# Gate of the first layer summed in one bank, and x1 turned over a diagonal, in a two-layer fp32 diffusion trunk

## The chip, the cores and the metric

The kernel runs on one core of one Trainium2 chip. The metric is the device time of one execution in microseconds, as a median of several runs. A profiled execution gives the trace; its times count from the start of its span.

## What is computed

Two layers work on 512 tokens of 1024 features in fp32. The first mixes tokens by averaging windows of 2, 4, 8 and 16 tokens, the second by a short gated convolution; after each comes a squared-ReLU MLP. Each sub-layer has an RMS norm before and after it, a shift and scale, and a gate; the six vectors of a layer are SiLU(c) times a 1024 x 6144 matrix, plus a bias.

```python
for i in range(DEPTH):                      # DEPTH = 2
    sh_m, sc_m, gt_m, sh_f, sc_f, gt_f = split(silu(c) @ ada_w[i] + ada_b[i], 6)
    h = rms_norm(x, norm_g[i, 0]) * (1 + sc_m) + sh_m
    y = pool_mixer(h) if i == 0 else short_conv_mixer(h)
    x = x + gt_m * rms_norm(y, norm_g[i, 1])          # "x1" in layer 0
    hf = rms_norm(x, norm_g[i, 2]) * (1 + sc_f) + sh_f
    x = x + gt_f * rms_norm(square(relu(hf @ ffn_w1[i])) @ ffn_w2[i], norm_g[i, 3])
```

## The kernel before

The engines' programs are written out by hand, each in one block; semaphores order them, and each engine runs its block strictly in the order written. So the order of calls in the code is the order on the engine.

Large products are made in three TensorE matmuls (`three`, lines 674 to 676): each fp32 operand is split into a high part, which ScalarE writes by a copy that rounds (`split_hi`, `first_hi`), and a low part, which VectorE makes by a subtraction (`split_lo`, `first_lo`). Weights come as units of 1 MB through two raw slots, by DMAs of the SP queue.

The change lies in the first 90 us or so, in which layer 0's mixer, its gate and the MLP's first inputs are made:

- **The modulation vectors.** `PRE` lists 20 loads of 1 MB of `ada_w[0]`, in order: eight for scale and shift of the mixer, four for the gate (numbers 8 to 11), eight for scale and shift of the MLP (12 to 19). Each load takes a quarter (256 columns) of one vector's 1024, for all 1024 input rows. A partition holds eight input rows, so its rows in memory are 1 KB. `PRE_SLOTS` says where in SBUF each load goes. `add_up(i)` multiplies load i by SiLU(c) on TensorE: eight matmuls, each with 32 output rows, four side by side. `SUMS` says which loads are summed into one PSUM bank; two banks (`sums_bank`) alternate.
- **The gate.** `gate_copy(part)` on VectorE adds bias and weight (`g_row`, which GpSimd prepares with a multiplication) to one quarter's sum; `turn_up(4 + part)` on TensorE spreads it over the partitions with the table `picks`; `group_gate(g)` on VectorE multiplies the quarter g of the mixer's output, for all tokens, by it.
- **The mixer.** `pool_group(g)` on TensorE makes the output of one group of 256 features, `group_out(g)` on VectorE copies it from PSUM to `y_tok`, `group_squares(g)` on ScalarE sums its squares. `split_lo(1)` on VectorE, the low part of the first MLP unit, stands between them.
- **x1 and its norm.** `first_x(t)` on VectorE makes x1 of tile t (128 tokens), `first_root(t)` on ScalarE its root mean square, `first_norm(t)` on VectorE multiplies all 1024 columns by the reciprocal and writes them to `y_tok`. `turn_first(side, pair)` on TensorE transposes four blocks of 128 x 128 of it (`nc.tensor.transpose`, line 955). It is called eight times, between `add_up`, `turn_up` and `part` in `start_pairs`.
- **The first inputs.** `first_input`, `first_hi` and `first_lo` scale, shift and split what was turned; `part(side, pair)` and `second_unit`, `third_unit` are the MLP's first products. `columns(n)` puts a quarter of scale and shift in place.
- **x stored.** `save_x(0)` on the SP queue writes x1 to memory before the load of unit 4; `load_x_parts`, which loads weights over `xs`, waits for it.
- `stay_busy` is six matmuls of a 128 x 128 identity that nobody reads.

Of the kernel before, what the change touches and what calls it, by code (L numbers as in the profile page):

```python
# [10 lines left out]
P = 128  # L11
# [77 lines left out]
PRE = ([(s, c) for c in range(4) for s in (SCALE_M, SHIFT_M)] + [(GATE_M, c) for c in range(4)]  # L89
# [3 lines left out]
SUMS = [(2 * c, 2 * c + 1) for c in range(4)] + [(PRE_GATE + c,) for c in range(4)] + [(PRE_F + 2 * c, PRE_F + 2 * c + 1) for c in range(4)]  # L93
# [42 lines left out]
def trunk(nc, x, c, ada_w, ada_b, norm_g, ffn_w1, ffn_w2, pool_w, pool_scale, conv_in_w, conv_w, conv_out_w, out):  # L136
    with ExitStack() as ctx:  # L137
# [60 lines left out]
        picks = sb("picks", [P, P])  # L198
# [37 lines left out]
        gate_bias = sem("gate_bias")  # L236
# [12 lines left out]
        x1_new, x1_sq, x1_rms, x1_rcp, x1_norm = sem("x1_new"), sem("x1_sq"), sem("x1_rms"), sem("x1_rcp"), sem("x1_norm")  # L249
# [33 lines left out]
        def pre_slot(i):  # L283
# [4 lines left out]
            return slot.rearrange("p (k n) -> p k n", k=NC)  # L288
# [234 lines left out]
        def _(sp):  # L523
# [15 lines left out]
            def load_pre(i):  # L539
# [10 lines left out]
                sp.dma_start(pre_slot(i), ada_rows(0)[:, :, seg * D + part * Q:seg * D + (part + 1) * Q]).then_inc(pre_in[PRE_SLOTS[i]], 16)  # L550
# [121 lines left out]
        def _(pe):  # L672
# [192 lines left out]
            def add_up(i):  # L865
# [20 lines left out]
            def turn_up(n):  # L886
                row = ada_rows_sb[:, n % 2, 0:Q]
                if is_gate(n):
                    part = n - 4
                    pe.wait_ge(gate_sums, part + 1)  # L890
                    if part >= 2:
                        pe.wait_ge(y0_gated, part - 1)
                    mm = nc.tensor.matmul(ps[:, 6 + part % 2, 0:Q], picks[:, :], row, start=True, stop=True)
                else:
                    pe.wait_ge(ada_row, cols_value(n))
                    for e in range(2):
                        mm = nc.tensor.matmul(ps[:, sums_bank(n), Q + 2 * e:Q + 2 * e + 2], row[:, e * P:(e + 1) * P], pick_two[:, :], start=True, stop=True)
# [44 lines left out]
            def turn_first(side, pair):  # L942
                pe.wait_ge(x1_norm, 2 * side + 2)
                pe.wait_ge(y0_gated, GROUPS)
# [8 lines left out]
                for n in range(2):  # L953
                    for t in range(2):
                        tr = nc.tensor.transpose(o[:, n, toks(t)], y_tok[:, 2 * side + t, (2 * pair + n) * P:(2 * pair + n + 1) * P], ident[:, :])
                tr.then_inc(x1_turned, 1)

            def start_pairs():
# [35 lines left out]
                turn_up(9)  # L994
                turn_first(1, 2)
                turn_up(10)
# [10 lines left out]
                turn_up(11)  # L1007
# [55 lines left out]
            turn_up(4)  # L1063
            pool_group(3)
            turn_up(5)
            add_up(10)
            add_up(11)
            turn_up(6)
            turn_up(7)
# [3 lines left out]
            turn_up(8)  # L1073
# [23 lines left out]
        def _(act):  # L1097
# [274 lines left out]
            copy_sums(11)  # L1372
# [46 lines left out]
        def _(dve):  # L1419
# [302 lines left out]
            dve.wait_ge(picks_step, 3)  # L1722
# [413 lines left out]
```

## Time and profile before

| | us |
|---|---|
| median of 3 runs | 938.18 (937.9 to 939.74) |
| the profiled execution | 937.01 |
| its span | 935.1 |
| TensorE busy in the span | 914.9 (98%) |
| VectorE busy | 649.3 (69%) |
| ScalarE busy | 431.1 (46%) |
| GpSimd busy | 53.2 (6%) |

The span is the time from the first to the last recorded instruction; 1.9 us of the profiled execution lie around it. The busy share of TensorE says little by itself, since the ends of matmuls are modelled: whether TensorE is the limit of a stretch is read from the starts of its matmuls and from what it waited for. DMA moves 170.86 MB in all, 41.88 MB of them in the first 140 us.

### The profile page before, as it was taken

The page shows a single profiled execution, that of the slowest core. Times are in us where ns is not written, and L with a number is a line of the kernel's source. Part 1 is how long each engine was busy: PE and PEld are TensorE (multiplying, and loading weights), DVE is VectorE, ACT ScalarE, POOL GpSimd, SP SyncE. Part 2 cuts the span into 40 slices and gives each one's busy share as a digit, 9 for nine tenths or more (in the row PEclk, how much of TensorE's full clock was granted, in tenths as well). Part 3 has the DMA queues.
Part 4 walks back from the last instruction along what each step waited for, and adds up shares of the span by engine and source line. Part 5 has one row for each costly group of instructions (what it writes and reads, how often), then busy time and mean ns, then how long its engine had stood idle before and what let it go on. Part 6 is the DMA issues. An engine that isn't in the chain of part 4 may idle for free.

```text
span 935.1 us, 11415 instructions
## 1 busy us (share of the span) xinstructions
PE 914.9 (98%) x4623; PEld 753.6 (81%) x4623; DVE 649.3 (69%) x622; ACT 431.1 (46%) x523; POOL 53.2 (6%) x83
## 2 busy tenths in 40 slices
PE   8889999999999999999999999999999999999996
PEld 6658888888888888889888888898888888888885
DVE  6786397589678866696766545757857864783688
ACT  6654484454346333354222224555634624543463
POOL 3002110010001001000101000000000000000001
PEclk9999999999999999999999999999999999999999
DMA  9999889527735576324656531273871661275124
GB/s 306 349 350 359 210 220 327 183 74 215 256 114 139 187 288 226 112 90 158 209 179 217 194 113 46 84 276 123 238 270 34 169 214 57 72 204 174 45 46 179
DMA packets 91403, 170.86 MB, mean 183 GB/s; under 512 B 4270, under 2 KB 34066, under 8 KB 91352
## 3 DMA queue, kind: packets, MB, share of 16 engines
q1 hardware_dynamic: 83912, 155.25, 48.5%
q0 software_dynamic: 7440, 14.89, 8.1%
q8 instruction: 36, 0.59, 0.3%
q14 instruction: 15, 0.12, 0.0%
HBM read 163.81 MB, written 6.32 MB: 182 GB/s over the span
## 4 chain that ended last, share of the span: by engine, by line
PE 52%; DVE 1%; issue 1%; ACT 0%; DVEq 0%
PE ps L674 17%; PE ps L676 17%; PE ps L675 17%; PE ps L768 1%; DVE y L1580 0%; DVE in_lo L1591 0%; PE ps L703 0%; DVE y L1945 0%; DVE xs L1956 0%; ACT in_hi L1209 0%; DVE y L1586 0%; DVE y L1474 0%; DVEq L137 0%; DVE y L1543 0%; DVE st L1949 0%
## 5 line engine op out<-in xcount | busy, mean ns | idle before, releaser
L674 PE MATMUL ps<-in_hi,w_parts 128*128 128x512 f32 (+1 forms) x784 | 290.1, 370 | 0.9 <-DVE in_lo L1591 0.5
L675 PE MATMUL ps<-in_lo,w_parts 128*128 128x512 f32 (+1 forms) x784 | 288.1, 367 | 0.0
L676 PE MATMUL ps<-in_hi,w_parts 128*128 128x512 f32 (+1 forms) x784 | 288.1, 367 | 0.0
L1422 DVE TENSOR_TENSOR w_parts<-raw,w_parts 128x2048 fp32r<-128x2048 f32 x81 | 185.5, 2290 | 125.5 <-ACT w_parts L1102 125.4
L1102 ACT ACTIVATE w_parts<-raw 128x2048 fp32r<-128x2048 f32 x81 | 154.8, 1911 | 214.4 <-PE ps L676 194.4
L674 PEld LDWEIGHTS ps<-in_hi,w_parts 128*128 128x128 f32 x784 | 147.8, 188 | 29.4 <-issue 3.3
L676 PEld LDWEIGHTS ps<-in_hi,w_parts 128*128 128x128 f32 x784 | 147.8, 188 | 24.5
L675 PEld LDWEIGHTS ps<-in_lo,w_parts 128*128 128x128 f32 x784 | 147.8, 189 | 24.1
L674 PE MATMUL ps<-w_parts,ops_hi 128*128 128x512 f32 x280 | 109.1, 389 | 0.2 <-DVE y L1474 0.2
L675 PE MATMUL ps<-w_parts,ops_hi 128*128 128x512 f32 x280 | 109.0, 389 | 0.0
L676 PE MATMUL ps<-w_parts,ops_lo 128*128 128x512 f32 x224 | 87.2, 389 | 0.0
L1432 DVE SCALAR_TENSOR_TENSOR ada_sum<-ada_raw,silu_t,ada_sum 128x1024 f32<-128x1024 f32 x56 | 71.7, 1281 | 4.7 <-DMA ada_raw<-in_ada_w_dram 2.2
L1112 ACT ACTIVATE work<-ps 128x512 f32<-128x512 f32 x56 | 33.3, 595 | 70.9 <-PE ps L676 70.9
L674 PEld LDWEIGHTS ps<-w_parts,ops_hi 128*128 128x128 f32 x280 | 52.6, 188 | 11.5 <-DVE y L1474 0.7
L675 PEld LDWEIGHTS ps<-w_parts,ops_hi 128*128 128x128 f32 x280 | 52.6, 188 | 10.9
L1474 DVE TENSOR_TENSOR y<-y,ps 128x512 f32<-128x512 f32 x82 | 52.9, 680 | 8.3 <-PE ps L676 8.3
L1422 DVE TENSOR_TENSOR w_parts<-xs,w_parts 128x2048 fp32r<-128x2048 f32 x21 | 48.0, 2285 | 3.3 <-ACT w_parts L1102 3.1
L1102 ACT ACTIVATE w_parts<-xs 128x2048 fp32r<-128x2048 f32 x21 | 40.3, 1919 | 21.6 <-PE ps L676 19.2
L674 PE MATMUL ps<-w_parts,mid_hi 128*128 128x512 f32 x128 | 50.1, 392 | 0.0
L676 PE MATMUL ps<-w_parts,mid_lo 128*128 128x512 f32 x128 | 49.8, 389 | 0.0
L675 PE MATMUL ps<-w_parts,mid_hi 128*128 128x512 f32 x128 | 49.8, 389 | 0.0
L676 PEld LDWEIGHTS ps<-w_parts,ops_lo 128*128 128x128 f32 x224 | 42.0, 188 | 8.7
(203 smaller groups left out, 1040.2 us busy)
## 6 DMA issues: line engine op xcount, KB each, us to landing
raw<-in_ffn_w_dram SPq DMA_DIRECT2D x57, 1024.0 KB, 5.5
ada_raw<-in_ada_w_dram SPq DMA_DIRECT2D x56, 512.0 KB, 6.2
xs<-in_ffn_w_dram SPq DMA_DIRECT2D x14, 1024.0 KB, 5.4
xs<-in_ffn_w_dram POOLq DMA_DIRECT2D x10, 1024.0 KB, 8.7
raw<-in_conv_in_w_dram SPq DMA_DIRECT2D x16, 512.0 KB, 5.3
raw<-in_ada_w_dram SPq DMA_DIRECT2D x4, 1024.0 KB, 11.1
ada_sum<-in_ada_w_dram SPq DMA_DIRECT2D x4, 1024.0 KB, 12.2
win<-in_ada_w_dram SPq DMA_DIRECT2D x4, 1024.0 KB, 11.9
```

What stands on the lines that cost most here:

```text
L674: nc.tensor.matmul(o, hi, b_hi, start=start, stop=False, skip_group_check=on)
L675: nc.tensor.matmul(o, hi, b_lo, start=False, stop=False, skip_group_check=on)
L676: return nc.tensor.matmul(o, lo, b_hi, start=False, stop=stop, skip_group_check=on)
L768: tr = nc.tensor.transpose(ps[:, at + n // 4, (n % 4) * P:(n % 4 + 1) * P], y_tok[:, t, n * P:(n + 1) * P], ident[:, :])
L1102: nc.scalar.activation(w_hi[:, u % W_SLOTS, :], raw_of(u), ACT.Copy).then_inc(w_hi_ready, 1)
L1112: nc.scalar.activation(work[:, n % 2, :], bank(p, m), ACT.Relu).then_inc(relu_done, 1)
L1422: nc.vector.tensor_tensor(w_lo[:, u % W_SLOTS, :], raw_of(u), w_hi[:, u % W_SLOTS, :].bitcast(F32), ALU.subtract).then_inc(w_lo_ready, 1)
L1432: nc.vector.scalar_tensor_tensor(out=ada_sum[:, s % 2, :], in0=ada_raw[:, i % ADA_SLOTS, :], scalar=silu_t[:, 3, k:k + 1], in1=ada_sum[:, ...
L1474: nc.vector.tensor_tensor(to, to, src, ALU.add if sign > 0 else ALU.subtract).then_inc(y_sum, 1)
```

## The change

Five things are changed.

1. The gate's four loads now take 256 of the 1024 input rows each, for all 1024 columns: `(GATE_M, kk)` is the pair of input rows `2*kk, 2*kk+1` of each partition, in rows of 4 KB. All four are summed in one bank, quarter j of the columns in the output rows from 32 j on. Four small matmuls add the bias to the sum at its start.
2. One VectorE operation (`weigh_gate`) multiplies the sum by the weight, after the fourth load; `spread_gate` on TensorE (four fp32 matmuls of 128 x 256) spreads it over banks 6 and 7; `token_gate(t)` on VectorE multiplies a tile of 128 tokens by it, over all 1024 columns. `gate_copy`, four of the `turn_up`, `group_gate`, `picks` and GpSimd's multiplication go.
3. `first_norm` becomes `first_diag`: the identity (128 columns) times the reciprocal. `turn_first` is now a matmul with a block of x1 as the stationary and this diagonal as the moving operand, so that it turns and scales in one.
4. On VectorE `first_x(3)` stands ahead of the first `columns` and `first_input`; on ScalarE `first_root(3)` ahead of `first_hi(0)`. `first_diag(2)` and `first_diag(3)` stand around `first_lo(0)`.
5. `save_x(0)` comes after the load of unit 4 and waits for all eight `turn_first`, which now read x1.

```diff
-PRE = (... + [(GATE_M, c) for c in range(4)] ...
+PRE = (... + [(GATE_M, kk) for kk in range(4)] ...
-SUMS = [...] + [(PRE_GATE + c,) for c in range(4)] + [...]
+SUMS = [...] + [tuple(range(PRE_GATE, PRE_F))] + [...]
...
+                if seg == GATE_M:
+                    sp.dma_start(pre_slot(i), ada_rows(0)[:, 2 * part:2 * part + 2, seg * D:(seg + 1) * D]).then_inc(pre_in[PRE_SLOTS[i]], 16)
...
+                if n == GATE_SUM:
+                    if first:
+                        pe.wait_ge(gate_row_in, 16)
+                        for j in range(4):
+                            nc.tensor.matmul(ps[32 * j:32 * (j + 1), sums_bank(n), 0:Q], ones[0:1, 0:32], gate_row[0:1, quarter(j)], start=True, stop=False)
+                    for k in range(2):
+                        for j in range(4):
+                            mm = nc.tensor.matmul(ps[32 * j:32 * (j + 1), sums_bank(n), 0:Q], silu_wide[:, 1, 2 * PRE[i][1] + k, :], pre_slot(i)[:, k, quarter(j)],
+                                                  start=False, stop=last and k == 1)
...
+            def spread_gate():
+                pe.wait_ge(gate_sums, 1)
+                pe.wait_ge(pool_diff, BAND_CHUNK + 2)
+                for j in range(4):
+                    mm = nc.tensor.matmul(ps[:, 6 + j // 2, (j % 2) * Q:(j % 2 + 1) * Q], ident[:, 32 * j:32 * j + 1].to_broadcast([P, P]), g_row[:, 0:Q], start=True, stop=True)
...
             def turn_first(side, pair):
-                pe.wait_ge(x1_norm, 2 * side + 2)
-                pe.wait_ge(y0_gated, GROUPS)
+                pe.wait_ge(x1_diag, 2 * side + 2)
+                pe.wait_ge(y0_gated, NT)
...
-                        tr = nc.tensor.transpose(o[:, n, toks(t)], y_tok[:, 2 * side + t, (2 * pair + n) * P:(2 * pair + n + 1) * P], ident[:, :])
+                        tr = nc.tensor.matmul(o[:, n, toks(t)], xs[:, 2 * side + t, (2 * pair + n) * P:(2 * pair + n + 1) * P], y_tok[:, 2 * side + t, 0:P], start=True, stop=True)
...
-            def gate_copy(part):
-                n = 4 + part
...
-                nc.vector.scalar_tensor_tensor(out=ada_rows_sb[:, n % 2, 0:Q], in0=ps[:, sums_bank(n), 0:Q], scalar=ident[:, 0:1],
-                                               in1=g_row[:, quarter(part)], op0=ALU.add, op1=ALU.mult).then_inc(gate_sums, 1)
+            def weigh_gate():
+                dve.wait_ge(ada_done, PRE_F)
+                dve.wait_ge(gate_g_in, 16 * 4)
+                nc.vector.tensor_tensor(g_row[:, 0:Q], ps[:, sums_bank(GATE_SUM), 0:Q], g_row[:, 0:Q], ALU.mult).then_inc(gate_sums, 1)
...
-            def group_gate(g):
...
+            def token_gate(t):
+                dve.wait_ge(ada_turned, GATE_SUM + 1)
+                dve.wait_ge(y0_sq, NT * (GROUPS - 1) + t + 1)
+                yt = y_tok[:, t, :].rearrange("p (a n) -> p a n", a=2)
+                nc.vector.tensor_tensor(yt, yt, ps[:, 6:8, :], ALU.mult).then_inc(y0_gated, 1)
...
-                nc.vector.tensor_scalar(y_tok[:, t, :], xs[:, t, :], st0[:, 7, t:t + 1], None, ALU.mult).then_inc(x1_norm, 1)
+                nc.vector.tensor_scalar(y_tok[:, t, 0:P], ident[:, :], st0[:, 7, t:t + 1], None, ALU.mult).then_inc(x1_diag, 1)
```

On TensorE, from the second half of the gate's sums to the wait for the first turn, the program before has (`L877` is `add_up`, `L893` and `L897` are `turn_up`, `L884` is `stay_busy`, `cu` holds SiLU(c) and the copied sums):

```order
L893 MATMUL ps<-cu,picks 128x256 [waits gate_sums]
L877 MATMUL ps<-mod_rows,cu 32x256 [waits gate_sums,pre_in3]
L877 MATMUL ps<-mod_rows,cu 32x256 x7
L877 MATMUL ps<-raw,cu 32x256 [waits gate_sums,pre_in6]
L877 MATMUL ps<-raw,cu 32x256 x7
L893 MATMUL ps<-cu,picks 128x256 [waits y0_gated,gate_sums] x2
L877 MATMUL ps<-win,cu 32x256 [waits gate_sums,pre_in7]
L877 MATMUL ps<-win,cu 32x256 x7
L877 MATMUL ps<-win,cu 32x256 [waits pre_in8]
L877 MATMUL ps<-win,cu 32x256 x7
L884 MATMUL ps<-ident,ones 128x128 x6
L897 MATMUL ps<-pick_two,cu 128x2 [waits ada_row]
```

The changed program has there, in the same place (`L883` is `add_up` of the gate, `L910` `spread_gate`):

```order
L883 MATMUL ps<-mod_rows,cu 32x256 [waits pre_in3]
L883 MATMUL ps<-mod_rows,cu 32x256 x7
L883 MATMUL ps<-raw,cu 32x256 [waits pre_in6]
L883 MATMUL ps<-raw,cu 32x256 x7
L910 MATMUL ps<-ada_raw,ident 128x256 [waits pool_diff,gate_sums]
L910 MATMUL ps<-ada_raw,ident 128x256 x3
L889 MATMUL ps<-win,cu 32x256 [waits cols_read,pre_in7]
L889 MATMUL ps<-win,cu 32x256 x7
L889 MATMUL ps<-win,cu 32x256 [waits pre_in8]
L889 MATMUL ps<-win,cu 32x256 x7
L896 MATMUL ps<-ident,ones 128x128 x6
L902 MATMUL ps<-pick_two,cu 128x2 [waits ada_row]
```

The four spreading matmuls of the gate, which stood apart, are now one group behind the last of its loads.

On VectorE, from the output of the third group to the first x1, the program before has (`L1800` is `group_out`, `L1795` `gate_copy`, `L1808` `group_gate`, `L1422` `split_lo(1)`, `L1813` `first_x`):

```order
L1800 TENSOR_TENSOR y<-ps,pool_row 128x4x256 [waits pool_done]
L1795 SCALAR_TENSOR_TENSOR cu<-ps,ident,ada_raw 128x256 [waits gate_g_in,gate_bias,ada_turned,ada_done]
L1808 TENSOR_TENSOR y<-y,ps 128x4x256 [waits y0_sq,ada_turned]
L1422 TENSOR_TENSOR w_parts<-raw,w_parts 128x2048 [waits w_hi_ready]
L1800 TENSOR_TENSOR y<-ps,pool_row 128x4x256 [waits pool_done]
L1808 TENSOR_TENSOR y<-y,ps 128x4x256 [waits y0_sq,ada_turned]
...
L1808 TENSOR_TENSOR y<-y,ps 128x4x256 [waits y0_sq,ada_turned]
L1883 RECIPROCAL st<-st 128x4 [waits y0_rms]
L1808 TENSOR_TENSOR y<-y,ps 128x4x256 [waits y0_sq,ada_turned]
L1813 SCALAR_TENSOR_TENSOR xs<-y,st,xs 128x1024 [waits y0_gated,y0_rcp] x3
```

The changed program has (`L1804` is `group_out`, `L1800` `weigh_gate`, `L1812` `token_gate`, `L1432` `split_lo(1)`, `L1817` `first_x`, `L1824` `first_diag`):

```order
L1804 TENSOR_TENSOR y<-ps,pool_row 128x4x256 [waits pool_done]
L1432 TENSOR_TENSOR w_parts<-raw,w_parts 128x2048 [waits w_hi_ready]
L1804 TENSOR_TENSOR y<-ps,pool_row 128x4x256 [waits pool_done]
L1800 TENSOR_TENSOR ada_raw<-ps,ada_raw 128x256 [waits gate_g_in,ada_done]
L1812 TENSOR_TENSOR y<-y,ps 128x1024 [waits y0_sq,ada_turned] x2
L1879 TENSOR_TENSOR st_y<-st_y 128x4x2 [waits y0_sq]
L1881 TENSOR_TENSOR st<-st_y 128x4 [waits y0_sum]
L1812 TENSOR_TENSOR y<-y,ps 128x1024 [waits y0_sq,ada_turned] x2
L1885 RECIPROCAL st<-st 128x4 [waits y0_rms]
L1817 SCALAR_TENSOR_TENSOR xs<-y,st,xs 128x1024 [waits y0_gated,y0_rcp] x3
L1822 RECIPROCAL st<-st 128x1 [waits x1_rms]
L1824 TENSOR_SCALAR y<-ident,st 128x128 [waits x1_rcp]
```

Two of the four multiplications by the gate stood before or beside the output of the last group; all four now stand behind it, and behind `weigh_gate`.

## Rows read from the trace of the kernel before

**Rows 1.** The page: busy time by engine.

```profile
PE 914.9 (98%) x4623; PEld 753.6 (81%) x4623; DVE 649.3 (69%) x622; ACT 431.1 (46%) x523; POOL 53.2 (6%) x83
```

**Rows 2.** Waits of PE (TensorE) from 110 to 420 us: total, times, longest.

```profile
PE ps L674 <- DVE y L1474: 0.2, 1, 0.2
```

**Rows 3.** Stretches: length, PE, PEld, DVE, ACT, POOL busy, clock, DMA share, GB/s.

```profile
79.00:90.00 11.00, 11.00 (x79) 9.28 (x78) 6.91 (x12) 3.76 (x4) 4.94 (x8) 1.00 0.96 368
...
40.00:55.00 15.00, 12.92 (x134) 8.89 (x123) 14.26 (x23) 10.29 (x31) 0.00 (x0) 1.00 1.08 350
84.00:86.00 2.00, 2.00 (x12) 1.68 (x10) 0.54 (x1) 1.43 (x3) 1.59 (x3) 1.00 1.01 409
...
6.00:8.00 2.00, 2.00 (x3) 0.76 (x3) 1.86 (x19) 1.96 (x4) 0.32 (x1) 1.00 1.03 416
```

**Rows 4.** Timeline of PE, gate to first turn: start, duration, line, records, [idle before].

```profile
50.41 0.59 PE L893 MATMUL ps<-cu,picks 128*128 128x256 f32 x2
...
52.77 1.07 PE L877 MATMUL ps<-raw,cu 128*32 128x256 f32 x16 [0.78 <-DMA raw<-in_ada_w_dram]
...
59.04 1.07 PE L877 MATMUL ps<-win,cu 128*32 128x256 f32 x16 [1.95 <-DMA win<-in_ada_w_dram]
60.04 1.60 PE L884 MATMUL ps<-ident,ones 128*128 128x128 f32 x12
61.83 0.61 PE L897 MATMUL ps<-pick_two,cu 128*128 128x2 f32 x4 [0.19 <-ACT cu L1273]
62.80 0.66 PE L955 MATMUL ps<-ident,y 128*128 128x128 f32 x4 [0.36 <-DVE y L1820]
```

**Rows 5.** Timeline of DVE (VectorE), same stretch and columns.

```profile
46.10 1.22 DVE L1800 TENSOR_TENSOR y<-ps,pool_row 128x1024 f32<-128x1024 f32 x1
...
51.07 1.22 DVE L1800 TENSOR_TENSOR y<-ps,pool_row 128x1024 f32<-128x1024 f32 x1
52.20 1.21 DVE L1808 TENSOR_TENSOR y<-y,ps 128x1024 f32<-128x1024 f32 x1
...
54.44 0.48 DVE L1795 SCALAR_TENSOR_TENSOR cu<-ps,ident,ada_raw 128x256 f32<-128x256 f32 x1
54.84 1.21 DVE L1808 TENSOR_TENSOR y<-y,ps 128x1024 f32<-128x1024 f32 x1
...
57.35 3.67 DVE L1813 SCALAR_TENSOR_TENSOR xs<-y,st,xs 128x1024 f32<-128x1024 f32 x3
...
61.99 0.75 DVE L1820 TENSOR_SCALAR y<-xs,st 128x1024 f32<-128x1024 f32 x1
```

**Rows 6.** Timeline of ACT (ScalarE): high part of unit 1, root of tile 1.

```profile
46.85 1.90 ACT L1102 ACTIVATE w_parts<-raw 128x2048 fp32r<-128x2048 f32 x1
...
61.21 0.30 ACT L1316 ACTIVATE st<-st,eps 128x1 f32<-128x1 f32 x1
```

**Rows 7.** Timeline of PE, first turns to the first whole unit; columns as in rows 4.

```profile
66.06 0.39 PE L674 MATMUL ps<-in_hi,w_parts 128*128 128x256 f32 x1
...
70.13 1.09 PE L955 MATMUL ps<-ident,y 128*128 128x128 f32 x8
71.16 1.07 PE L877 MATMUL ps<-win,cu 128*32 128x256 f32 x16
...
82.94 0.50 PE L674 MATMUL ps<-in_hi,w_parts 128*128 128x512 f32 x1
```

**Rows 8.** Timeline of PE: one window of the mixer, four plain fp32 matmuls.

```profile
17.72 1.18 PE L927 MATMUL ps<-bands,xn_tok 128*128 128x132 f32 x8
18.83 1.07 PE L877 MATMUL ps<-y,cu 128*32 128x256 f32 x16
```

**Rows 9.** Timeline of PE at the end: its last matmul.

```profile
926.23 0.39 PE L676 MATMUL ps<-w_parts,ops_lo 128*128 128x512 f32 x1
```

**Rows 10.** A stretch behind it, columns as in rows 3.

```profile
931.00:932.00 1.00, 0.00 (x0) 0.00 (x0) 0.96 (x4) 0.00 (x0) 0.00 (x0) 0.68 0.69 258
```

**Rows 11.** Timeline of the SP queue: the loads that wait for the store of x.

```profile
89.33 1.06 SPq L621 DMA_DIRECT2D xs<-in_ffn_w_dram  x2
```

More of the change, by code:

```diff
@@ L887, in turn_up @@
                 row = ada_rows_sb[:, n % 2, 0:Q]
[L888 to L897, printed above, removed]
+                pe.wait_ge(ada_row, cols_value(n))
+                for e in range(2):
+                    mm = nc.tensor.matmul(ps[:, sums_bank(n), Q + 2 * e:Q + 2 * e + 2], row[:, e * P:(e + 1) * P], pick_two[:, :], start=True, stop=True)
+                mm.then_inc(ada_turned, 1)
+            def spread_gate():
+                pe.wait_ge(gate_sums, 1)
+                pe.wait_ge(pool_diff, BAND_CHUNK + 2)
+                for j in range(4):
+                    mm = nc.tensor.matmul(ps[:, 6 + j // 2, (j % 2) * Q:(j % 2 + 1) * Q], ident[:, 32 * j:32 * j + 1].to_broadcast([P, P]), g_row[:, 0:Q], start=True, stop=True)
                 mm.then_inc(ada_turned, 1)
@@ L1006, in start_pairs @@
                 second_unit(2)
-                turn_up(11)
+                turn_up(8)
                 second_unit(3)
@@ L1062, in _ @@
             add_up(9)
-            turn_up(4)
             pool_group(3)
-            turn_up(5)
             add_up(10)
             add_up(11)
-            turn_up(6)
-            turn_up(7)
+            spread_gate()
             add_up(PRE_F)
@@ L1072, in _ @@
             stay_busy(0, 6)
-            turn_up(8)
+            turn_up(5)
             ffn(0)
@@ L1371, in _ @@
             split_hi(3)
-            copy_sums(11)
+            copy_sums(8)
             first_hi(4)
@@ L1750, in columns @@
             def columns(n):
-                part = n % 4
-                late = n >= 8
+                late = n > GATE_SUM
+                part = n - GATE_SUM - 1 if late else n
                 c = slice(2 * part, 2 * part + 2)
@@ L1863, in _ @@
             diff_lo(5)
-            gate_copy(0)
             diff(6)
@@ L1869, in _ @@
             group_out(2)
-            gate_copy(1)
-            group_gate(0)
             split_lo(1)
             group_out(3)
-            group_gate(1)
-            gate_copy(2)
+            weigh_gate()
+            token_gate(0)
+            token_gate(1)
             dve.wait_ge(y0_sq, NT * GROUPS)
@@ L1879, in _ @@
             nc.vector.tensor_tensor(st0[:, 2, :], st_y[:, :, 0], st_y[:, :, 1], ALU.add).then_inc(y0_sum, 1)
-            gate_copy(3)
-            group_gate(2)
+            token_gate(2)
+            token_gate(3)
             dve.wait_ge(y0_rms, 1)
             nc.vector.reciprocal(st0[:, 4, :], st0[:, 3, :]).then_inc(y0_rcp, 1)
-            group_gate(3)
             first_x(0)
@@ L1887, in _ @@
             first_x(2)
-            first_norm(0)
-            first_norm(1)
-            columns(8)
+            first_diag(0)
+            first_diag(1)
+            first_x(3)
+            columns(5)
             first_input(0)
+            first_diag(2)
             first_lo(0)
-            first_x(3)
-            first_norm(2)
-            first_norm(3)
+            first_diag(3)
             first_input(1)
-            columns(9)
+            columns(6)
             first_lo(1)
@@ L1901, in _ @@
             first_lo(2)
-            columns(10)
+            columns(7)
             first_input(3)
@@ L1907, in _ @@
             split_lo(3)
-            columns(11)
+            columns(8)
             first_input(5)
```

68 lines of the change are left out of this document (27 added, 41 removed).

## The prediction

> **What bounds the kernel now.** I read the page first: TensorE is busy 98% of the span [rows 1]. Its waits come next, since busy time alone proves nothing here: from 110 to 420 us it waits 0.2 us in all [rows 2], and from 79 to 90 us it has no idle time [rows 3]. So from the first turn of x1, at 62.80 us [rows 4], TensorE runs without a gap, and two things decide the time: **when that turn starts, and how much TensorE has to do behind it**. Ahead of it two others set the pace. The 16 DMA engines are full, 350 GB/s at a share of 1.08 from 40 to 55 us [rows 3]; TensorE waits 0.78 us for the last load of the gate and 1.95 us for load 13 [rows 4]. And VectorE is busy 14.26 of these 15 us [rows 3]. The chain into the first turn is: add_up of the last gate load at 52.77 [rows 4], its copy at 54.44, the third and fourth multiplication by the gate from 54.84 on, first_x from 57.35 on [rows 5], the root of tile 1 until 61.51 [rows 6], its norm until 62.74 [rows 5], the turn at 62.80 [rows 4].
>
> **The loads.** A load is 1.05 MB. At 350 GB/s it takes 3.00 us. No row shows 4 KB rows alone; the nearest are the stretch with x's own loads, which have rows of 4 KB, at 416 GB/s, and one with weights in rows of 2 KB and the store of x, at 409 [rows 3]. At 409 a load takes 2.56 us, so the fourth gate load lands 4 x 0.44 = 1.8 us sooner, at about 51.0. Bounds: nothing gained (52.7), or 1.9 us at 416. Not all of it can be used. pool_group(3) holds TensorE until 50.4 (the next matmul starts at 50.41 [rows 4]), add_up(10) follows, 1.0 us, so add_up(11) starts at 51.4 instead of 52.77 and is done at 52.45. The bias matmuls, at most 0.5 us by add_up's 16 records in 1.07 [rows 4], stand ahead of pool_group(2) and push it by 0.1. GpSimd's multiplication and `picks` go from work that nobody waits for: nothing.
>
> The Trainium skill (DMA: Bandwidth & Descriptors, "Where 436 GB/s comes from") has it that transfers from HBM are held at about 358 GB/s by the HBM's side, whatever their rows. The trace does not agree: 409 and 416 in two stretches of full DMA [rows 3]. By that rule the loads would gain nothing, and the end would lie 1.4 us later than my sum.
>
> **The gate's way to x1.** This is the first term that costs. group_out(2) ends at 47.3 as before, since it follows pool_group(2) [rows 5]. split_lo(1) follows ScalarE's high part, which ended at 48.75 [rows 6] and may come 0.4 sooner; so group_out(3) ends at about 51.9. Then VectorE has nothing to do until the sum is complete: weigh_gate at 52.5, priced as gate_copy's 0.48 [rows 5], ends at 52.95. spread_gate is four fp32 matmuls of 256 columns. One is two records and takes 0.59 with its tail [rows 4]; a record of 128 columns takes 0.13 (twelve in 1.60 [rows 4]), one of 256 at that pace 0.26, and eight 2.1; ready at 55.15 with the waits between. Only now can any tile be gated. From group_out to group_gate is 1.13 us (51.07 to 52.20) [rows 5], and token_gate has their size: four take 4.5. The two small sums and the reciprocal I put at 0.7 with their waits. first_x(0) starts at **60.35, against 57.35** [rows 5]: 3.0 later. Seen from the end of add_up(11), the way to first_x took 3.5 us (53.84 to 57.35) and takes 7.9, and it begins 1.4 us sooner: two multiplications that had been done early now stand behind the wait, and the spread is 1.6 longer.
>
> From there first_x and first_root run as before, so the root of tile 1 ends at 61.51 + 3.0 = 64.5. The diagonal is shorter than the norm, which took 0.75 for 1024 columns [rows 5]; 128 columns I put at 0.2, between nothing and 0.75, and both diagonals are ready at 64.95. But turn_up(5) stands ahead of the turn on TensorE and waits for ScalarE's copy behind the same root: 64.83 instead of 61.83 [rows 4]; it takes 0.5. The first turn starts at 65.3 instead of 62.80: **+2.5 us**. Bounds: +1.5, if spread and gates overlap better than that, and +3.9, if the loads gain nothing.
>
> **The turn over a diagonal.** A transpose was one record a block: eight take 1.03 us (70.13 to 71.16) [rows 7], 0.129 each, and a turn of four 0.53 with its waits. A plain fp32 matmul is two records. The mixer's windows have the very form of the new turn, a 128 x 128 fp32 block standing and 131 to 135 fp32 columns moving, and their eight records take 1.11 us from start to start [rows 8]; stay_busy's twelve take 1.60 [rows 4]. I take 1.05 us for a turn of four. All eight turns lie where TensorE doesn't wait, two ahead of part(0,0), six behind: 8 x 0.52 = **+4.2 us**. Bounds: 3.4 (0.12 a record, stay_busy without its tail) and 4.7 (the windows' pace).
>
> The Trainium skill (TensorE: Matmul & The Clock Gate, "Terms") says that the transpose mode is four times faster for FP32. By that a turn would take 2.1 us and the term would be 12.6 us, 953 in all. The windows show twice, not four times [rows 8], and I go by them; to the other I give a chance of 0.01.
>
> **Who else could be late.** first_x(3) ahead of the first input costs VectorE 1.2 us at 65, while TensorE turns until 66.4: first_input(0) follows at 66.7, first_hi(0) behind the root of tile 3 at 67.7, first_lo(0) is done at 69.0. TensorE comes to part(0,0) at 69.4 (65.3, two turns 2.1, two add_up 2.0), against 66.06 [rows 7], so nothing waits; behind it the longer turns are themselves the cover. On the SP queue unit 4's load now goes ahead of the store of x, which waits for the last turn, about 86, and lands near 92 (2 MB at 409 GB/s). load_x_parts waits for it. It was issued at 89.33 [rows 11], and the load ahead of it on the queue waits for split_lo(3), which moves along with TensorE by 6.7: about 96. Free; if the store took 5 us longer, still about free, as DMA is idle there part of the time and TensorE has had nothing to wait for behind 110 [rows 2].
>
> **Sum.** 2.5 + 4.2 = +6.7 us, carried to the end in full, as no gap of TensorE behind could take it up; second_unit's start goes from 82.94 [rows 7] to 89.6. On the profiled execution, 937.0, that makes 943.7. The median of the runs shown lies 1.2 above it, so the forecast is **944.9**.
>
> **Rivals.**
> 1. *The clock falls in a new gap.* Before, TensorE's longest gap from 50 us to the first turn is 1.95 us [rows 4]. In the new order stay_busy ends near 59.9 (load 13 lands at 57.3, add_up 1.0, stay_busy 1.6) and turn_up(5) waits until 64.8: 4.9 us of nothing. At the end of the trace the clock fell from the 2.4 to the 1.2 GHz level within the microsecond from 931 (mean 0.68 [rows 10]), some 4.7 us after the last matmul's end [rows 9]. Three to four us of work at the lower level cost 1.5 to 2: 946.5 to 947. For it: the two gaps are about equal. Against: for that very reason it may as well not fall. The Trainium skill (TensorE: Matmul & The Clock Gate, "Why this matters for your kernels") warns of such gaps. Chance 0.25.
> 2. *VectorE and ScalarE set the pace from 66 to 83.* They scale and split the first inputs between the turns, and TensorE's records may hold waits too short to show. Then half of the second passes is hidden: 2.5 + 2.1, 942.8. Against: two turns follow each other at 0.129 a record [rows 7], no slower than stay_busy, which waits for nothing. Chance 0.12.
> 3. *Faster.* If the gate were ready when group_out(3) ends, at 51.9 and not 55.15, VectorE would go through without a wait and with three copies (1.3) and two long norms (1.1) less; the first turn would start 2.4 us sooner, and if a turn cost no more than a transpose, the time would be 935.8. It takes both: a sum 3 us earlier than DMA at 409 GB/s gives it, and rows 8 not holding for the turn. Chance 0.05.
> 4. *It cancels.* A start 2 to 4 us sooner by the same mechanism, with turns at full price: 936.5 to 940. Chance 0.05.
>
> **Numbers.** The forecast itself has 0.52. Slower by over 0.2% (1.9 us, about what a measurement of this kernel tells from no change) are the forecast, rivals 1 and 2 and the page's rule, 0.90; within it rival 4, 0.05; faster 0.05. The range reaches down to the low ends of both terms with part of rival 2 (1.5 + 3.4 on 938.2 is 943.1, less 2.1), 941, and up to rival 1 with the high price of the turns, 948.5.
>
> **What would show it.** Right: VectorE idle for 3 us ahead of token_gate, which starts at 55; first_x at 60.3; the first turn at 65.3; two records a block and 1.05 us a turn; second_unit at 89.6. Wrong: token_gate from 52 on; one record a block; gaps of TensorE between 69 and 90. A granted clock below 1 at about 65 us would be rival 1.

## The result, and the profile after

| | before | after |
|---|---|---|
| median of the runs | 938.04 us | 947.72 us |
| lowest and highest | 937.9, 939.74 | 946.4, 949.05 |
| profiled execution, its span | 937.0, 935.1 | 946.4, 944.5 |

The ratio is 1.0095, with a 95% interval from 1.0078 to 1.0111: the changed kernel is slower by 9.7 us. The forecast was +6.7 (944.9) with a range up to 948.5.

The page of the changed kernel, busy time by engine, against [rows 1]:

```profile
PE 921.0 (98%) x4663; PEld 760.4 (81%) x4663; DVE 645.3 (68%) x618; ACT 431.1 (46%) x523; POOL 51.1 (5%) x84
```

TensorE has 40 records more. The eight turns bring 32 of them (four blocks each, one record more a block), the bias matmuls of the gate the other 8. The waits of TensorE from 110 to 420 us, against [rows 2], where there were 0.2 us:

```profile
PE ps L674 <- DVE y L1484: 0.9, 1, 0.9
```

The timeline of TensorE, against [rows 4] and [rows 7] (start, duration, line, records, idle time before). `L883` is `add_up` of the gate, `L910` `spread_gate`, `L889` `add_up` of the rest, `L896` `stay_busy`, `L902` `turn_up`, `L968` `turn_first`, `L674` the first line of a part:

```profile
41.45 0.63 PE L880 MATMUL ps<-gate_row,ones 1*32 1x256 f32 x8
...
52.50 1.07 PE L883 MATMUL ps<-raw,cu 128*32 128x256 f32 x16 [0.85 <-DMA raw<-in_ada_w_dram]
54.12 1.99 PE L910 MATMUL ps<-ada_raw,ident 128*128 128x256 f32 x8 [0.55 <-DVE ada_raw L1800]
...
58.53 1.07 PE L889 MATMUL ps<-win,cu 128*32 128x256 f32 x16 [1.42 <-DMA win<-in_ada_w_dram]
59.53 1.60 PE L896 MATMUL ps<-ident,ones 128*128 128x128 f32 x12
65.65 0.62 PE L902 MATMUL ps<-pick_two,cu 128*128 128x2 f32 x4 [4.52 <-ACT cu L1283]
66.14 2.05 PE L968 MATMUL ps<-y,xs 128*128 128x128 f32 x8
68.12 1.73 PE L889 MATMUL ps<-ada_raw,cu 128*32 128x256 f32 x16
69.78 1.16 PE L968 MATMUL ps<-y,xs 128*128 128x128 f32 x8
...
71.87 0.39 PE L674 MATMUL ps<-in_hi,w_parts 128*128 128x256 f32 x1
...
91.54 0.50 PE L674 MATMUL ps<-in_hi,w_parts 128*128 128x512 f32 x1
```

Three things are to be seen. The last load of the gate, and with it everything behind, comes later than I had it: the first turn starts at 66.14, not at 65.3. Ahead of `turn_up` TensorE has a gap of 4.52 us. And the same work is long behind it: a turn of eight records takes 2.05 us the first time and 1.16 the second, an `add_up` of 16 records 1.73 and not 1.07. The stretches (length, PE, PEld, DVE, ACT, POOL busy, granted clock, DMA share, GB/s) say why:

```profile
60.00:65.00 5.00, 1.14 (x11) 0.94 (x9) 4.93 (x7) 2.48 (x5) 0.00 (x0) 1.00 1.10 348
66.00:67.00 1.00, 1.00 (x7) 1.00 (x7) 1.00 (x2) 0.93 (x3) 0.00 (x0) 0.55 1.09 347
...
66.00:70.00 4.00, 4.00 (x29) 2.71 (x28) 2.77 (x9) 3.00 (x7) 0.00 (x0) 0.57 1.08 363
70.00:75.00 5.00, 5.00 (x52) 4.16 (x55) 0.97 (x3) 0.98 (x2) 0.00 (x0) 1.00 1.07 355
```

The granted clock falls to 0.5, the 1.2 GHz level, at about the first turn behind the gap, and the mean of 0.57 over these 4 us makes 3.4 us at that level. That is rival 1.

The timeline of VectorE, against [rows 5] (`L1804` `group_out`, `L1800` `weigh_gate`, `L1812` `token_gate`, `L1817` `first_x`, `L1824` `first_diag`):

```profile
50.73 1.22 DVE L1804 TENSOR_TENSOR y<-ps,pool_row 128x1024 f32<-128x1024 f32 x1
53.64 0.42 DVE L1800 TENSOR_TENSOR ada_raw<-ps,ada_raw 128x256 f32<-128x256 f32 x1 [1.69 <-PE ps L883]
56.15 2.35 DVE L1812 TENSOR_TENSOR y<-y,ps 128x1024 f32<-128x1024 f32 x2 [2.09 <-PE ps L910]
...
61.17 3.68 DVE L1817 SCALAR_TENSOR_TENSOR xs<-y,st,xs 128x1024 f32<-128x1024 f32 x3
...
65.56 0.29 DVE L1824 TENSOR_SCALAR y<-ident,st 128x128 f32<-128x128 f32 x1
```

VectorE waits 1.69 us for the sum and 2.09 for the spread, 3.8 in all, in a stretch where it had been busy nearly throughout [rows 3]. Put together, the profiled execution's 9.4 us of span are: the first turn 3.34 later (62.80 to 66.14); the turns longer by 3.7; the low clock 1.5; and 0.7 of a wait at 164 us that wasn't there. The turns: from part(0,0) to `second_unit`, where the clock is full again, it takes 19.67 us (71.87 to 91.54) against 16.88 [rows 7], 2.79 for six turns or 0.465 each, and 8 x 0.465 = 3.7. The clock: from the first turn to part(0,0) it takes 5.73 us against 3.26 [rows 4, 7], 2.47, of which two turns account for 0.93.

### The profile page after: what moved, and what is told of

Its sections match the earlier page's. It is cut to its first block, busy times and chain, and to the rows that moved or that the text cites. A ratio compares the mean times of both kernels' runs of the same rounds, so it can differ in the third digit from the quotient of the medians.

```text
span 944.5 us, 11480 instructions
## 1 busy us (share of the span) xinstructions
PE 921.0 (98%) x4663; PEld 760.4 (81%) x4663; DVE 645.3 (68%) x618; ACT 431.1 (46%) x523; POOL 51.1 (5%) x84
## 4 chain that ended last, share of the span: by engine, by line
PE 52%; DVE 1%; issue 1%; ACT 0%; DVEq 0%
PE ps L674 17%; PE ps L676 17%; PE ps L675 17%; PE ps L768 1%; DVE y L1590 0%; DVE in_lo L1601 0%; PE ps L703 0%; DVE y L1946 0%; DVE xs L1957 0%; ACT in_hi L1219 0%; DVE y L1596 0%; DVE y L1484 0%; DVEq L138 0%; DVE y L1553 0%; DVE st L1950 0%
## 5 line engine op out<-in xcount | busy, mean ns | idle before, releaser
L674 PE MATMUL ps<-in_hi,w_parts 128*128 128x512 f32 (+1 forms) x784 | 290.1, 370 | 0.9 <-DVE in_lo L1601 0.4
L1432 DVE TENSOR_TENSOR w_parts<-raw,w_parts 128x2048 fp32r<-128x2048 f32 x81 | 185.5, 2290 | 128.2 <-ACT w_parts L1112 128.0
L674 PEld LDWEIGHTS ps<-in_hi,w_parts 128*128 128x128 f32 x784 | 147.8, 189 | 29.2 <-issue 3.7
L674 PE MATMUL ps<-w_parts,ops_hi 128*128 128x512 f32 x280 | 109.1, 389 | 0.9 <-DVE y L1484 0.9
L674 PEld LDWEIGHTS ps<-w_parts,ops_hi 128*128 128x128 f32 x280 | 52.6, 188 | 12.3 <-DVE y L1484 1.3
L1432 DVE TENSOR_TENSOR w_parts<-xs,w_parts 128x2048 fp32r<-128x2048 f32 x21 | 48.0, 2284 | 4.0 <-ACT w_parts L1112 3.8
L674 PE MATMUL ps<-w_parts,mid_hi 128*128 128x512 f32 x128 | 50.1, 392 | 0.0
```

What stands on the lines that cost most here:

```text
L674: nc.tensor.matmul(o, hi, b_hi, start=start, stop=False, skip_group_check=on)
L1432: nc.vector.tensor_tensor(w_lo[:, u % W_SLOTS, :], raw_of(u), w_hi[:, u % W_SLOTS, :].bitcast(F32), ALU.subtract).then_inc(w_lo_ready, 1)
```

## Experiments

All were compared with the kernel before on the same chip. Its medians there were 939.12 (first four), 939.15 (next four) and 938.29 (last four).

### The parts apart: the diagonal alone, the gate alone

`e2_diag_only` is the kernel before with the turns over a diagonal, and the store behind the load of unit 4:

```diff
-                        tr = nc.tensor.transpose(o[:, n, toks(t)], y_tok[:, 2 * side + t, ...], ident[:, :])
+                        tr = nc.tensor.matmul(o[:, n, toks(t)], xs[:, 2 * side + t, ...], y_tok[:, 2 * side + t, 0:P], start=True, stop=True)
-                nc.vector.tensor_scalar(y_tok[:, t, :], xs[:, t, :], st0[:, 7, t:t + 1], None, ALU.mult).then_inc(x1_norm, 1)
+                nc.vector.tensor_scalar(y_tok[:, t, 0:P], ident[:, :], st0[:, 7, t:t + 1], None, ALU.mult).then_inc(x1_diag, 1)
```

> The kernel before with the diagonal alone: first_norm becomes the diagonal, turn_first a plain matmul from xs, and the store of x stands behind the load of unit 4 and waits for the last turn; gate, loads and order as before. Theory A (a plain fp32 turn costs TensorE twice the records, 0.46 us more a turn as measured in the changed kernel): 8 x 0.46 = 3.7 us more, less about 0.4 for a diagonal ready sooner than the norm, so 941.3. Theory B (the turns are hidden and the loss is all in the gate): 938, or 0.4 less.

Measured: 942.53 us, ratio 1.0045 (1.0027 to 1.0063), +3.4. Its timeline of TensorE shows two turns behind each other at a full clock:

```profile
71.17 2.05 PE L956 MATMUL ps<-y,xs 128*128 128x128 f32 x16
73.16 1.07 PE L878 MATMUL ps<-win,cu 128*32 128x256 f32 x16
```

Two turns take 1.99 us, 0.995 each, where before two took 1.03 (70.13 to 71.16 [rows 7]): 0.48 more a turn, a factor of 1.9. The term is confirmed, slightly under my 0.52. TensorE also waits for VectorE longer here than in the kernel before, which has 0.2 us at the same place [rows 2] (from 60 to 420 us):

```profile
PE ps L675 <- DVE y L1475: 1.3, 2, 0.9
```

`e4_gate_only` is the kernel before with the gate's part alone (points 1 and 2 of the change). `e3_norm` is the changed kernel with norm and transposes back, so with points 4 and 5 beside the gate:

```diff
-                nc.vector.tensor_scalar(y_tok[:, t, 0:P], ident[:, :], st0[:, 7, t:t + 1], None, ALU.mult).then_inc(x1_diag, 1)
+                nc.vector.tensor_scalar(y_tok[:, t, :], xs[:, t, :], st0[:, 7, t:t + 1], None, ALU.mult).then_inc(x1_norm, 1)
```

> The kernel before with the gate's part alone: loads by rows of 4 KB, one bank, weigh_gate, spread_gate, token_gate; transposes, order of first_x(3) and store of x as before. Theory A (the gate's way moves the first turn by 3.3 us and drops the clock, 1.5 us): 938.0 + 3.3 + 0.4 + 1.5 = about 943, and within 1 us of the run with the diagonal undone, as order and store cost next to nothing. Rival (order of first_x(3) costs 1 us or more): it would be over 1 us faster than that run. If the gate's part were free: 938.

> The changed kernel with the diagonal undone: norm over 1024 columns and transposes as before; gate in one bank, order and store as changed. Theory A: 3.7 us less for the turns, 0.4 more for the norm ahead of the first turn: about 944.4, with the gap and the fall of the clock still there. If instead the turns cost nothing, 947.7 or a little more.

Measured: 943.49 us for the gate alone, ratio 1.0048 (1.0031 to 1.0066), +4.4; 943.33 with points 4 and 5, ratio 1.0056 (1.0034 to 1.0078), +4.2. So these runs show no cost of the earlier first_x(3) and the later store on top of the gate, within intervals of 3 to 4 us. The same gap stands in the gate alone (timeline of TensorE):

```profile
66.34 1.01 PE L901 MATMUL ps<-pick_two,cu 128*128 128x2 f32 x4 [4.52 <-ACT cu L1282]
67.31 1.11 PE L967 MATMUL ps<-ident,y 128*128 128x128 f32 x4
```

A turn of four transposes, 0.66 before [rows 4], takes 1.11 behind it. The diagonal's 3.4 and the gate's 4.4 sum to 7.8, under the 9.7 of both.

### Point 4 alone

`e5_x3_only` is the kernel before with first_x(3) and first_root(3) earlier:

```diff
+            first_x(3)
             columns(8)
             first_input(0)
+            first_norm(2)
             first_lo(0)
-            first_x(3)
-            first_norm(2)
             first_norm(3)
```

> The kernel before with part 4 alone: first_x(3) ahead of the first columns and first_input on VectorE, first_root(3) ahead of first_hi(0) on ScalarE. My theory: nothing is late by it, since TensorE comes to part(0,0) only after two turns and two add_up; here the first turn is at 62.8 and part(0,0) at 66.1, so first_lo(0), which comes 1.2 us of VectorE later, could hold it by up to 1 us: 0 to +1 us against the kernel before. Rival: the order itself costs 2 us or more, and the near equality of the kernel with norm and transposes and of the gate alone was chance.

Measured: 939.59 us, ratio 1.0011 (1.0001 to 1.0021), +1.3 by the medians and +1.0 by the ratio. The theory named 0 to +1, and its waits show the very one that it named:

```profile
PE ps L674 <- DVE in_lo L1841: 0.8, 1, 0.8
```

Part(0,0) waits for first_lo(0). The changed kernel has no such wait, with the low clock or without it (`after`, `e8_again`): two longer turns bring TensorE there later. That the point costs nothing there is cover, as the forecast said, and not a property of the edit.

### The gap and the clock

`e1_busy` is the changed kernel with `stay_busy(0, 20)` for `stay_busy(0, 6)` ahead of `turn_up(5)`:

> The changed kernel with stay_busy(0, 20) in place of stay_busy(0, 6) ahead of the turn_up that waits for ScalarE; nothing else is touched. Theory A (part of the loss is the clock that falls in the 4.5 us gap of TensorE before the first turn): the clock stays at its upper level in the stretch from 60 to 75 us, the turn at 68 us takes 1.0 us for eight records instead of 2.0, and the time falls by 1.5 us, to about 946.2. Theory B (the slow stretch from 66 to 70 comes from the longer waits around it, the clock only marks it): the time stays at 947.7.

Measured: 944.75 us, ratio 1.0065 (1.0047 to 1.0084), +5.6. The unchanged `after_again`, below, measured +9.5 on the same chip, so this kernel is clearly faster. But its profile shows that the clock fell all the same, behind a gap of only 1.41 us (timeline, then stretches):

```profile
60.32 4.73 PE L896 MATMUL ps<-ident,ones 128*128 128x128 f32 x40
66.46 0.61 PE L902 MATMUL ps<-pick_two,cu 128*128 128x2 f32 x4 [1.41 <-ACT cu L1283]
66.93 1.61 PE L968 MATMUL ps<-y,xs 128*128 128x128 f32 x8
```

```profile
67.00:68.00 1.00, 1.00 (x8) 1.00 (x8) 0.98 (x3) 0.86 (x4) 0.00 (x0) 0.72 1.11 350
68.00:70.00 2.00, 2.00 (x19) 0.84 (x18) 1.51 (x5) 1.73 (x4) 0.00 (x0) 0.50 1.09 360
```

So the clock fell in this execution in spite of the filling. It is the slowest of the four (946.23 us at a mean clock of 0.993; the others have 943.56 to 945.32 at 0.996 and 0.997), and what the clock did in the others isn't recorded: the kernel doesn't price it. The next one fills the gap with wide matmuls, `e8_fill`, beside the unchanged `after_again` on the same chip:

```diff
             stay_busy(0, 6)
+            for i in range(5):
+                nc.tensor.matmul(ps[:, 0, :].rearrange("p (a n) -> p a n", a=4), ones[:, :], ident[:, :].unsqueeze(1).to_broadcast([P, 4, P]), start=True, stop=True)
             turn_up(5)
```

> The changed kernel once more, unaltered, on the same chip as the three runs beside it. The separate runs priced the diagonal at 3.4 us and the gate's part at 4.4, 7.8 in sum, and the changed kernel measured 9.7. If the parts add and the first run of the changed kernel met the low clock more often than the parts did, this one lies at +8 to +9.5 us over the kernel before; if both parts together cost something of their own, at +9.7 or more.

> The changed kernel with five matmuls of 512 columns of the identity behind stay_busy, ahead of the turn_up that waits for ScalarE: TensorE is filled with long matmuls until about 65.4 us, with short ones it fell to the lower clock all the same in one profile. Theory A (the clock before the first turn is worth 1.5 to 3 us): no stretch between 60 and 75 us at the lower level, the first turns at 1.0 us for eight records, and 1.5 to 3 us less than the changed kernel beside it. Theory B (the clock costs nothing): equal to it. If the fill ends too late it adds its overhang, at most 0.5 us.

Measured: 948.65 us for the changed kernel again, ratio 1.0103 (1.009 to 1.0116), +9.5; 945.37 with the filling, ratio 1.007 (1.0057 to 1.0082), 3.3 less. Stretches of the first, then of the second, where the first turn starts at 69.60 and at 68.67 (both later than the 66.14 above, as the clock had also fallen earlier: means of 0.83 from 20 to 40 us in the first, from 10 to 20 and from 50 to 60 us in the second):

```profile
69.00:70.00 1.00, 1.00 (x6) 1.00 (x7) 1.00 (x2) 0.97 (x3) 0.00 (x0) 0.56 1.10 349
70.00:71.00 1.00, 1.00 (x6) 1.00 (x6) 0.58 (x4) 0.89 (x2) 0.00 (x0) 0.50 1.10 347
```

```profile
68.00:72.00 4.00, 3.80 (x40) 2.96 (x44) 3.50 (x11) 3.56 (x9) 0.00 (x0) 1.00 1.07 372
```

The gate alone was run again with and without the same five matmuls, together with the filled kernel once more: `e4_again`, `e9_gate_fill`, `e8_again`.

> The gate part alone once more, as the base of the next kernel on the same chip: +4.4 us against the kernel before, as it was, with a granted clock of about 0.5 behind the gap of 4.5 us ahead of turn_up(5).

> The gate part alone, with five more plain fp32 matmuls of 512 columns between stay_busy and turn_up(5), 4.46 us of work whose result nobody reads. Theory (the clock that falls in the gap is a term of its own, and the late gate costs only its delay): 2 to 3 us less than the gate part alone, so +1.5 to +2.5 against the kernel before, and with it the parts add up: about 2 for the gate and 3.4 for the diagonal and under 1 for the last wait make the 6.2 measured for the changed kernel with the same filling. Rival (the clock is a side show, and the gate's order costs the 4.4 by itself): no change, +4.4.

> The changed kernel with the same five matmuls once more, for the difference of diagonal and norm at a clock that stays up, on one chip: +6.2 us against the kernel before as it was, and 3.5 to 4.5 above the gate part with the filling. If the parts didn't add up for another reason than the clock, this difference would stay near 5, as between the changed kernel and the gate part alone.

| kernel | median | ratio (95% interval) | above before |
|---|---|---|---|
| e4_again | 944.22 | 1.0073 (1.0051 to 1.0096) | +5.9 |
| e9_gate_fill | 942.30 | 1.0044 (1.0028 to 1.0060) | +4.0 |
| e8_again | 944.45 | 1.0073 (1.0056 to 1.0090) | +6.2 |

`e4_again` was expected at +4.4 and came out at +5.9, the same kernel as `e4_gate_only`. The filling takes 1.9 us from the gate alone by the medians, in overlapping intervals; I had expected 2 to 3, and the level of +4.0 lies above the 1.5 to 2.5 named. The difference of 2.15 between the filled kernels misses its 3.5 to 4.5. The last two misses have the same look: the four runs of `e9_gate_fill` are 940.53 and 941.42 at a mean clock of 0.998, and 943.18 and 943.8 at 0.994. The profiled one is of the second kind. Its clock is full where the turns are, and low for a part of the time from 10 to 20 us; the same stretch of the gate alone is the third row:

```profile
68.00:73.00 5.00, 4.64 (x52) 3.05 (x53) 3.84 (x8) 2.28 (x5) 0.00 (x0) 1.00 1.08 365
```

```profile
10.00:20.00 10.00, 7.79 (x65) 5.88 (x63) 4.43 (x8) 5.63 (x9) 0.00 (x0) 0.83 1.09 347
```

```profile
67.00:73.00 6.00, 6.00 (x44) 3.26 (x44) 4.45 (x10) 2.77 (x6) 0.00 (x0) 0.50 1.08 365
```

Such falls in the first 60 us come and go from one execution to the next. The one profile of the kernel before has none in its first 110 us; its runs' mean clocks go from 0.990 to 0.998. Runs with a mean clock of 0.997 or 0.998 compare best. The five of the kernel before on this chip have a median of 938.4 (937.5 to 938.6), the filled gate 940.5 and 941.4, the filled changed kernel 944.0, 944.2 and 944.7. That gives +2.6 for the late gate and 3.2 more for the diagonal, which alone had measured +3.4. At a full clock the parts then add up. This rests on two and three runs, and in the kernel before a lower mean clock doesn't always mean a longer time (938.3 at 0.992), so it is an estimate; the medians alone don't decide it. Nor do they show that the parts fail to add up: 3.4 and the 5.9 of `e4_again` make 9.3, against 9.5 and 9.7.

The price of the clock behind the gap is read more sharply in the profiles, as the time from the first turn to part(0,0). At a full clock it is 4.15 us with the diagonal (`e8_fill`, `e8_again`) and 3.26 with transposes (the kernel before; 3.18 in `e9_gate_fill`):

| profile | gap ahead of `turn_up` | first turn to part(0,0) | above a full clock |
|---|---|---|---|
| after | 4.52 | 5.73 | 1.6 |
| after_again | 4.53 | 5.51 | 1.4 |
| e6_queue | 4.71 | 5.80 | 1.6 |
| e1_busy | 1.41 | 5.72 | 1.6 |
| e4_gate_only | 4.52 | 5.30 | 2.0 |
| e3_norm | 4.51 | 5.62 | 2.4 |
| e4_again | 4.53 | 5.82 | 2.6 |
| e7_all | 1.27 | 4.75 | 1.5 |

The first four have the diagonal, the last four transposes. So 1.4 to 1.6 us of the 3.3 between `after_again` and `e8_fill` are this price, as far as their profiles show it. The rest isn't explained; falls of the clock elsewhere can be in it.

### The loads

`e6_queue` puts the third load of the gate ahead of unit 1's load on the SP queue, and unit 1's splits later, so that the buffers stay free of each other:

```diff
-            for i in range(2, 10):
+            for i in range(2, 11):
                 load_pre(i)
             load(1)
-            for i in range(10, PRE_F + 6):
+            for i in range(11, PRE_F + 6):
                 load_pre(i)
...
             group_out(2)
-            split_lo(1)
             group_out(3)
             weigh_gate()
+            split_lo(1)
             token_gate(0)
```

> The changed kernel with load 10 (third of the gate) ahead of the load of unit 1 on the SP queue, the high part of unit 1 behind group_squares(2) on ScalarE, its low part behind weigh_gate on VectorE, where VectorE waited. Theory A (the faster gate loads brought only 0.3 us because the load of unit 1 waits for add_up(7) until 40.5 us and the queue runs dry behind the loads 8 and 9): no dip of DMA at 41 us, add_up of the last gate load at about 51.5 instead of 52.5, and about 1 us less in all. Rival (rows of 4 KB aren't faster than rows of 1 KB): add_up of it stays at 52.5 and the time too.

Measured: 947.3 us, ratio 1.0094 (1.0079 to 1.0108), +8.15, which is 1.35 less than the changed kernel on the same chip; the two intervals overlap, so the time alone doesn't prove a gain, and it is the starts in the trace that show one. The stretches of the changed kernel show what it mends:

```profile
38.00:40.00 2.00, 2.00 (x24) 1.63 (x27) 0.55 (x1) 1.34 (x4) 0.00 (x0) 1.00 1.04 418
...
41.00:42.00 1.00, 1.00 (x12) 0.59 (x12) 0.72 (x4) 0.00 (x0) 0.00 (x0) 1.00 0.73 213
42.00:43.00 1.00, 1.00 (x20) 0.42 (x16) 0.95 (x3) 0.98 (x2) 0.00 (x0) 1.00 0.98 252
...
44.00:46.00 2.00, 2.00 (x18) 1.94 (x17) 1.78 (x3) 2.00 (x7) 0.00 (x0) 1.00 1.07 420
46.00:48.00 2.00, 1.59 (x22) 0.89 (x21) 1.23 (x1) 2.00 (x5) 0.00 (x0) 1.00 1.02 414
```

Rows of 4 KB do run at 418 and 414 GB/s (38 to 40 and 46 to 48 us), faster than my 409; the kernel before has 345 and 356 there. The 420 between them are of rows of 2 and 4 KB together. But the load of unit 1 stands in the SP queue until TensorE has added up the eighth load, and is issued at 40.47 only (timeline of the SP queue):

```profile
40.47 0.37 SPq L596 DMA_DIRECT2D raw<-in_ffn_w_dram  x1
```

In the kernel before it was issued at 40.51. So what the first two loads of the gate had gained is lost in front of it: the loads ahead land sooner, and the DMA engines run short of work, 213 and 252 GB/s from 41 to 43 us (before: 314 and 260). With the order of `e6_queue` it is 397 and 416, and the forecast's own times appear: the sum at 51.22 (forecast 51.4), the first turn at 65.25 (65.3):

```profile
51.22 1.05 PE L883 MATMUL ps<-raw,cu 128*32 128x256 f32 x16
...
64.37 1.02 PE L902 MATMUL ps<-pick_two,cu 128*128 128x2 f32 x4 [4.71 <-ACT cu L1283]
65.25 2.06 PE L968 MATMUL ps<-y,xs 128*128 128x128 f32 x8
```

### What is best of both

`e7_all` takes the order of loads of `e6_queue`, the norm and transposes of `e3_norm`, and four wide filling matmuls:

> The changed kernel with everything mended that was found: norm and transposes as before instead of the diagonal (-3.7), the queue kept full and the splits moved (-1.0), four long fill matmuls (-1.5 to -3), a norm 0.4 longer. Expected: 9.0 - 3.7 - 1.0 - 2 + 0.4 = about 2.7 us over the kernel before. It can't beat it, if the theory is right that the gate is multiplied in behind its sum and all four times there. Rival (the gate in one bank is worth having once the rest is mended): at or below the kernel before.

Measured: 941.3 us, ratio 1.0031 (1.0019 to 1.0043), +2.15. With an edit against every loss that was found, the new gate is still behind the old one. What is left is in its timeline of TensorE, the first turn at 65.52 against 62.80 [rows 4], and in the stretch behind it, where the clock fell in spite of the filling:

```profile
59.68 3.60 PE L1084 MATMUL ps<-ident,ones 128*128 128x512 f32 x8
64.55 0.61 PE L902 MATMUL ps<-pick_two,cu 128*128 128x2 f32 x4 [1.27 <-ACT cu L1285]
65.52 0.66 PE L968 MATMUL ps<-ident,y 128*128 128x128 f32 x4 [0.36 <-DVE y L1826]
```

```profile
67.00:70.00 3.00, 3.00 (x28) 1.31 (x20) 2.85 (x7) 2.20 (x5) 0.00 (x0) 0.50 1.06 375
```

The 2.72 us of the later turn and the 1.5 of the clock make up the 4.2 by which this profile's span (939.3) exceeds that of the kernel before. So the clock wasn't mended in that execution, and how much of the +2.15 is the clock isn't shown. Its two runs with a mean clock of 0.998 took 940.83 and 941.16 us, those of the kernel before on this chip 937.71 and 938.1: about 3 us remain there too.

No kernel tried beats the one before.

## Why the prediction was right, and where it was short

The sign and the mechanism were right: the first turn starts later, the turns are longer, and all of it reaches the end. The size was 6.7 for 9.7. The time lies within the range because the upper end, 948.5, had been set by rival 1 and a high price of the turns. The turns came in 0.5 us under their term, and the range happened to have room for two things that the prediction didn't have: a start later by 0.84 us, and a wait of 0.7.

- **The loads: the step failed.** I let the fourth load of the gate land 1.8 us sooner and the sum start at 51.4. The rate was right (414 to 418 GB/s for my 409), but the sum started at 52.50, 0.27 sooner than before. I priced the loads at a rate and didn't follow the queue: which load waits for which sum, once those ahead of it are shorter. `e6_queue` shows it, with the sum at 51.22. By the start of the first turn it is worth 0.89 us; the medians say 1.35, with intervals that overlap.
- **The gate's way to x1: right.** From the sum's start to first_x I had 8.95 us (51.4 to 60.35); the trace has 8.67 (52.50 to 61.17). From there to the first turn 4.95 and 4.97. The diagonal took 0.29 for my 0.2, the spread 1.92 for my 2.1 (its eight records, 54.12 to 56.04).
- **The first turn:** +3.34 for +2.5, within the bounds of +1.5 to +3.9, and the whole of the excess is the loads.
- **The turns over a diagonal: right, a little under.** 0.465 to 0.48 each for 0.52, 3.7 in all for 4.2. The windows of the mixer [rows 8] were the right rows. The Trainium skill (TensorE: Matmul & The Clock Gate, "Terms") has the transpose mode four times faster for FP32; the trace has a factor of 1.9 for this turn, and the 953 that would follow from four was not reached.
- **Rival 1: it happened, on top of the forecast's case.** I gave it 0.25 and 1.5 to 2 us. The profiles with the diagonal lose 1.4 to 1.6 to it, as priced; those with transposes and the same gap 2.0 to 2.6, where the low stretch is longer (in `e4_again` all of 67 to 73 us). The medians differ by 3.3 (`after_again` against `e8_fill`) and 1.9 (`e4_again` against `e9_gate_fill`), and hold more than this one fall. I had seen the gap to 0.4 us (4.9, measured 4.52) and had a row of a fall behind a gap of 4.7 [rows 9, 10], and argued that near equality spoke as much against. That was the error of judgement: the row showed a fall, and I named none in which the clock had stood through such a gap. In all six profiles with a gap of 4.5 to 4.7 us there, it fell.
- **Rival 2** didn't happen: behind the first turn TensorE has no gap in 60 to 110 us, and the term of the turns came in nearly full.
- **Rivals 3 and 4** would have needed the gate ready at 51.9; `token_gate` started at 56.15.
- **The store: free, as said.** It was issued at 87.76, and `load_x_parts` at 96.91 behind a load on the queue that waited until 96.49; I had 96. The Trainium skill (DMA: Bandwidth & Descriptors, "Where 436 GB/s comes from") gives about 358 GB/s as what binds transfers from HBM, and derives it as a core's half of what two cores share; it says nothing of rows. This kernel runs on one core, and with 414 to 418 GB/s in this trace the measurement decides. What a second core would leave of that, no run here shows.
- **"No gap behind could take it up": true, and one was added.** Part of the 9.4 us of span is the wait at 164 us, 0.9 where there was 0.2 at 155. It stands in `e2_diag_only` (1.3), `e6_queue` (1.1), `after_again` (0.9), `e8_fill` (0.8) and `e8_again` (0.5), all with the diagonal; with transposes it is 0 to 0.5 (`e3_norm` and `e4_gate_only` none, `e7_all` 0.2, `e9_gate_fill` 0.3, `e4_again` 0.5). But `e1_busy` has the diagonal and no such wait. What makes it stays open; no kernel was made for it.

The sum with what was measured: 3.3 for the start, 3.7 for the turns, 1.5 for the clock and 0.7 for the late wait give 9.2, for 9.4 us of span and 9.7 by the medians.

## What to carry to other kernels

In this kernel faster loads brought little as long as the next one on their queue couldn't be issued sooner: after pricing the rate, follow the queue and find the load that waits for a consumer. When an edit opens a gap on TensorE ahead of work that sets the end, price the clock as part of the forecast and not beside it, if the trace holds one fall behind a gap of that length; and look whether a filling of the gap kept the clock, before counting on it. And a step that is free may be so only because another loss in the same change covers it, as point 4 was: alone it costs about 1 us (0.1 to 2 by its interval).

## What was not expected of the hardware

- Filling the gap didn't keep the clock each time. It fell behind 40 records of 128 columns in 4.73 us and a gap of 1.41 us (`e1_busy`), and behind 8 records of 512 columns in 3.60 us and a gap of 1.27 (`e7_all`). It stood behind 10 records of 512 columns in 4.46 us, with a gap of 1.56 in `e8_fill` and of 0.24 in `e8_again` and `e9_gate_fill`. So neither the width of the matmuls alone nor the length of the gap alone sorts these five executions, and the cause isn't settled.
- The stretch at the low level behind the gap differs between kernels and executions: 3.4 us in the changed kernel, nearly 7 in `e4_again`. One profile doesn't give that price.
- Plain fp32 matmuls of 128 x 128 by 128 cost 1.9 times the transposes of the same blocks.
